# A two-layer block, attention and routed experts in float32: the last three weight passes walked once per 128-token tile

## The reference

```python
def mixer_sublayer(h, w_in, ...):
    proj = h @ w_in                    # 2048 x 7176
    sb_q, sb_k, sb_v, fq, fk, fv, fgate, flogit = jnp.split(proj, ...)
    sb = stick_breaking_attention(...)      # 8 heads of 128, causal
    fox = forgetting_attention(rms_norm(fq), rms_norm(fk), fv, log_f)  # 8 heads, causal
    merged = jnp.concatenate([rms_norm(sb, sb_out_gain),
                              rms_norm(fox, fox_out_gain) * jax.nn.sigmoid(fgate)], axis=-1)
    return merged @ w_out              # 2048 x 2048
...
def peer_sublayer(h, w_query, sub_keys, u, v):
    def block(hb):                     # 128 tokens
        q = (hb @ w_query).reshape(PEER_BLOCK, PEER_HEADS, 2, D_KEY // 2)   # 2048 x 2048
        s = jnp.einsum('thpc,hpnc->thpn', q, sub_keys)
        top_s, top_i = lax.top_k(s, PEER_TOPK)
        ...                            # 16 experts of 16384 for each token and head
        u_sel = jnp.take(u, idx, axis=0)
        a = jax.nn.gelu(jnp.einsum('thkd,td->thk', u_sel, hb), approximate=False)
        v_sel = jnp.take(v, idx, axis=0)
        return jnp.einsum('thk,thkd->td', g * a, v_sel)
    return lax.map(block, blocks)
```

## Time and profile before

| | before |
|---|---|
| time, median of 3 runs | 3122.51 us (3119.54, 3122.51, 3128.95) |
| span of the profiled execution | 3121.8 us |
| busy: TensorE, VectorE, ScalarE, GpSimd | 2089.0, 1836.5, 853.8, 800.9 us |
| second w_in (p4), loads issued | from 1141.1 us, for 508 us |
| query pass (p6), loads issued | from 1739.3 us, for 122 us |
| first gather of experts | 1797.4 us |
| last expert product on TensorE | starts at 3110.9 us |

### The profile page before, as it was taken

How to read it: one execution, slowest core, us unless ns; L and a number is a source line. 1 busy time by engine, 2 the same in 40 slices (tenths; PEclk the granted TensorE clock), 3 DMA queues, 4 the chain that set the end, 5 groups by cost and what they waited for, 6 DMA issues and landing times.

```text
span 3121.8 us, 29077 instructions
## 1 busy us (share of the span) xinstructions
PE 2089.0 (67%) x11378; PEld 1478.6 (47%) x11378; DVE 1836.5 (59%) x2711; ACT 853.8 (27%) x1267; POOL 800.9 (26%) x680
## 2 busy tenths in 40 slices
PE   5888989989999999999999983223232322322235
PEld 2676777888787787666668871000000000000001
DVE  3679886566776664343336697766565555564430
ACT  1334544444454454544545420000000000000000
POOL 1111110000000000000000036665555555555552
PEclk8999999999999999999999996566656566666667
DMA  9887875557665545334226699999999999999998
GB/s 385 289 293 263 296 259 150 184 182 248 210 189 153 164 158 172 111 122 132 85 82 201 194 377 403 422 422 421 421 422 421 422 421 419 421 421 421 421 421 346
DMA packets 244741, 900.90 MB, mean 289 GB/s; under 512 B 20759, under 2 KB 45613, under 8 KB 178413
## 3 DMA queue, kind: packets, MB, share of 16 engines
q0 software_dynamic: 94208, 612.85, 48.9%
q1 hardware_dynamic: 149152, 284.53, 27.8%
q10 hardware_dynamic: 1244, 1.67, 0.2%
HBM read 894.78 MB, written 2.10 MB: 287 GB/s over the span
## 4 chain that ended last, share of the span: by engine, by line
PE 45%; DMA 29%; DVE 10%; ACT 3%; issue 3%; POOL 2%; ACTq 0%; POOLq 0%; DVEq 0%
PE pp L1818 38%; DMA late<-in_peer_v,MI 9%; DMA P<-in_peer_v,MI 5%; PE tp L1818 5%; DMA x<-in_peer_v,MI 5%; DMA ring<-in_peer_v,MI 4%; DVE wL L1130 3%; DMA SY<-in_peer_v,MI 2%; PE tp L1821 2%; ACT wH L626 1%; DMA ring<-in_peer_w_query 1%; DVE UHM L1286 1%; DMA ring<-in_w_in 1%; POOL late L2361 1%; DVE P L1777 0%
## 5 line engine op out<-in xcount | busy, mean ns | idle before, releaser
L1130 DVE TENSOR_TENSOR wL<-ring,wH 128x1024 fp32r<-128x1024 f32 (+3 forms) x504 | 583.2, 1161 | 573.7 <-ACT wH L626 572.4
L1818 PE MATMUL pp<-wH,hH 128*128 128x512 f32 (+3 forms) x1888 | 745.7, 395 | 35.5 <-DVE wL L1130 19.4
L1818 PE MATMUL pp<-wL,hH 128*128 128x512 f32 (+3 forms) x1888 | 721.4, 382 | 0.0
L1818 PE MATMUL pp<-wH,hL 128*128 128x512 f32 (+3 forms) x1888 | 720.5, 382 | 0.0
L626 ACT ACTIVATE wH<-ring 128x1024 fp32r<-128x1024 f32 (+3 forms) x504 | 508.3, 1011 | 729.7 <-PE pp L1818 548.0
L1818 PE MATMUL pp<-late,S 128*32 128x512 f32 x768 | 232.6, 879 | 335.7 <-DMA x<-in_peer_v,MI 156.3
L1818 PEld LDWEIGHTS pp<-wH,hH 128*128 128x128 f32 x1888 | 362.3, 192 | 141.2 <-issue 46.3
L1818 PEld LDWEIGHTS pp<-wH,hL 128*128 128x128 f32 x1888 | 361.6, 192 | 64.1
L1818 PEld LDWEIGHTS pp<-wL,hH 128*128 128x128 f32 x1888 | 362.8, 192 | 57.3 <-issue 1.0
L1777 DVE CUSTOM_DVE_ANT_0 late<-late,P 128x2048 f32<-128x2048 f32 x84 | 191.2, 2288 | 155.2 <-DMA late<-in_peer_u,MI 155.2
L1818 PE MATMUL pp<-P,S 128*32 128x512 f32 x360 | 162.7, 898 | 166.9 <-DMA late<-in_peer_v,MI 93.2
(11 more groups left out here) (305 smaller groups left out, 2985.2 us busy)
## 6 DMA issues: line engine op xcount, KB each, us to landing
ring<-in_w_in SPq DMA_DIRECT2D x288, 512.0 KB, 4.4
ring<-in_w_out SPq DMA_DIRECT2D x96, 512.0 KB, 4.2
P<-in_w_mod POOLq DMA_DIRECT2D x85, 512.0 KB, 5.1
late<-in_w_mod SPq DMA_DIRECT2D x64, 512.0 KB, 9.4
SY<-in_w_mod POOLq DMA_DIRECT2D x43, 512.0 KB, 5.5
ring<-in_w_in SPq DMA_DIRECT2D x48, 368.0 KB, 4.8
ring<-in_peer_w_query SPq DMA_DIRECT2D x32, 512.0 KB, 7.9
ring<-in_w_in SPq DMA_DIRECT2D x24, 344.0 KB, 3.2
```

What stands on the lines that cost most here:

```text
L1130: tt(lo, raw, hi.bitcast(F32), ALU.subtract).then_inc(*tick("dve_lo", *names))
L1818: return e.matmul(o, l, r, start=start, stop=stop, skip_group_check=skip)
```

## The change

The first block stays. In the second block, tile 0 and tile 1 part:

- **Pass 1** (p4 to p6) computes only tile 0 (and the meta tokens). Pieces are now 128 rows of up to 1024 columns: still 512 KB, in rows of 4 KB. Of every four pieces of 128 rows one (`pc % 4 == 2`) is plain: TensorE reads it as float32 from the ring, against unsplit activations `hP` in `P`. The other three are split as before. A plain piece's ring buffer is free only when TensorE has used it.
- **Pass 2** (p7 to p9) loads w_in, w_out and the query matrix again, for tile 1, and every piece is plain. The tile's keys, values and activations are computed here; ScalarE and VectorE split no weights.
- **Beside pass 2** stand the 128 gathers and dots of tile 0's u, in 6 slots: `dot(SHARE)` after each piece adds 0.68 of a gather. The choices of groups 0 to 3 are laid into pass 2's attention. The rest of the experts (128 gathers of u for tile 1, 256 of v) comes after pass 2, in 13 slots.
- The attention code works tile by tile, so tile 0's queries meet one tile of keys. The sub-key load (2 x 512 KB) is done twice.

The core of the diff:

```diff
-G_IN2 = cgroups((FG + 688, 1, 344), *[(c + 512 * h, 1, 512) for h in range(2) for c in (SQ, SK, SV, FQ, FK, FV)],
-                (FG, 2, 344))
-GROUPS = [G_IN, G_OUT, G_IN, G_OUT, G_IN2, G_OUT, G_OUT]
-PIECES = [[(n, c0, w, pc) for n, (c0, w) in enumerate(g) for pc in range(8)] for g in GROUPS]
-NB, NS, NG = 3, 4, 11
-FIRST_DOT = 12
+G_IN2 = [(FG + 688, 344), (FQ, 1024), (FK, 1024), (FV, 1024), (FG, 688), (SQ, 1024), (SK, 1024), (SV, 1024)]
+G_OUT2 = [(0, 1024), (1024, 1024)]
+GROUPS = [G_IN, G_OUT, G_IN, G_OUT, G_IN2, G_OUT2, G_OUT2, G_IN2, G_OUT2, G_OUT2]
+BOTH = 4
+NPC = [8] * BOTH + [16] * 6
+PIECES = [[(n, c0, w, pc) for n, (c0, w) in enumerate(g) for pc in range(NPC[p])] for p, g in enumerate(GROUPS)]
+NB, NS, NG = 3, 4, 13
+SHARE = 0.68
...
+def row_of(p, n, pc):
+
+    return (pc + 8) % 16 if (p in (4, 7) and n == 7) or (p in (5, 8) and n == 0) else pc
+
+
+def plain(p, q):
+
+    return p >= 7 or (p >= BOTH and PIECES[p][q][3] % 4 == 2)
...
+    dots, chosen = [0, 0.0], [0]
+
+    def dot(share):
+        dots[1] += share
+        while dots[1] >= 1:
+            dots[1] -= 1
+            if dots[0] < 32 * min(chosen[0], 4):
+                yield "dot", dots[0] // 32, dots[0] % 32
+                if dots[0] >= 32 and dots[0] % 32 == 3:
+                    yield "gelu", dots[0] // 32 - 1
+                dots[0] += 1
...
+    for p in (4, 7):
+        t, share = tile_of(p), 0 if p == 4 else SHARE
+        for q, (n, c0, w, pc) in enumerate(PIECES[p]):
+            yield from splits(p, q)
+            if p == 4:
+                if n == 0 and pc == 4:
+                    yield "norm", 4
+                if n and pc == 3:
+                    yield "drain", "M"
+                if meta_part(c0, w):
+                    yield "meta", p, q
+            elif n == 0 and pc in (1, 2, 4, 6):
+                yield ("turn_q", 6, 1) if pc == 1 else ("scores", pc // 2)
+            elif (n, pc) in ((1, 2), (1, 14), (2, 10)):
+                yield from choice({(1, 2): 2, (1, 14): 3, (2, 10): 4}[n, pc])
+            if p == 7 and (n, pc) == (0, 8):
+                yield from choice(1)
+            yield "piece", p, q
...
+            yield from pump(*((0.8, 0.8, 1) if p == 4 else (0.7, 0.7, 1)))
+            yield from dot(share)
...
+                for k in range(14 if t else 0):
+                    yield "step", "X"
+                    yield "step", "Y"
+                    yield from dot(1)
+                yield "drain", "X", "Y"
...
+    yield "rest",
+    yield "turn_q", 9, 1
+    yield "scores", 6
+    yield "scores", 7
+    yield "open", "X", "choose", 4
+    yield "blend", 0
+    for b in range(8):
+        yield "vmix", 0, b
+        yield from dot(4)
+        yield from pump(1.5, 0, 0)
+    while dots[0] < 128:
+        yield from dot(1)
+        yield from pump(1, 0, 0)
+    yield "gelu", 3
...
-            had, queue = {}, [0, 1, 2, 3, 4]
-            for n in range(512):
-                if n == 34 - FIRST_DOT:
-                    queue = list(range(5, NG)) + queue
-                i = queue.pop(0)
-                queue.append(i)
-                yield i, had.get(i)
-                had[i] = n
+            had, queue, n = {}, [0, 1, 2, 3, 4, 5], 0
+            for what, *a in order():
+                if what == "rest":
+                    queue = list(range(6, NG)) + queue
+                for _ in range({"dot": 1, "vmix": 4}.get(what, 0)):
+                    i = queue.pop(0)
+                    queue.append(i)
+                    yield i, had.get(i)
+                    had[i] = n
+                    n += 1
...
+                    if p < BOTH:
+                        load(W[p][pc * 256:(pc + 1) * 256, c0:c0 + wd].rearrange("(k p) n -> p k n", p=128), 2, wd)
+                    else:
+                        k = row_of(p, n, pc)
+                        load(W[p][k * 128:(k + 1) * 128, c0:c0 + wd].unsqueeze(1), 1, wd)
...
+            def piece_one(p, q):
+                n, c0, wd, pc = PIECES[p][q]
+                whole, r, kk = plain(p, q), raw_of[p, q], row_of(p, n, pc)
+                k = None if whole else next(cut)
+                w.wait_ge(*(at("raw", r) if whole else at("lo", k)))
+                w.wait_ge(*(at("plain", p, kk // 4) if whole and p < 7 else at("chunk", p, kk // 4)))
+                h = hP if p < 7 else hB
+                for j, (o, wj) in enumerate(sides(wd)):
+                    b = bank_of(p, n, j)
+                    if pc == 0 and b in had_bank:
+                        w.wait_ge(*at(*had_bank[b]))
+                    if not whole:
+                        m = three(pp[b][:, 0:wj], (hA[0][:, kk, :], hA[1][:, kk, :]),
+                                  (wH[k % NB][:, o:o + wj], wL[k % NB][:, o:o + wj]), pc == 0, pc == 15)
+                    else:
+                        m = mm(pp[b][:, 0:wj], h[:, kk, :], ring[:, r % NS, o:o + wj], pc == 0, pc == 15)
+                    names = []
+                    if o + wj == wd:
+                        if not whole:
+                            names.append(("cut used", k))
+                        elif not (p == 4 and meta_part(c0, wd)):
+                            names.append(("ring used", r))
+                    if pc == 15:
+                        names.append(("grouped", p, n, j))
+                        had_bank[b] = ("bank free", p, n, j)
+                    m.then_inc(*tick("pe_piece", *names))
...
                 if before is not None:
                     w.wait_ge(*at("expert used", before))
-                elif slot in (3, 4):
+                elif slot < 6:
+                    w.wait_ge(*at("grouped", 6, 1, 1))
+                elif slot in (7, 8):
+                    w.wait_ge(*at("fox out", 1, 0, 1))
+                    w.wait_ge(*at("fox out", 1, 1, 1))
+                elif slot in (9, 10):
                     w.wait_ge(*at("turned x"))
-                    w.wait_ge(*at("hidden", slot - 3))
-                elif slot == 5:
-                    w.wait_ge(*at("lo", LAST_CUT))
-                elif slot == 7:
-                    w.wait_ge(*at("grouped", 6, 3))
+                    w.wait_ge(*at("hidden", slot - 9))
+                else:
+                    w.wait_ge(*at("grouped", 9, 1, 1))
...
```

More of the change, by code:

```diff
@@ L620, in split @@
                 n, c0, wd, pc = PIECES[p][q]
-                r, k = next(loads), next(cut)
-                raw = heads(ring[:, r % NS, 0:2 * wd], 2)
+                r = next(loads)
+                if plain(p, q):
+                    return
+                k, size = next(cut), 2 * wd if p < BOTH else wd
                 w.wait_ge(*at("raw", r))
@@ L988, in forget @@
[L988 to L999 removed]
+                half = meta[1]
@@ new lines, in turn_four @@
+                u = next(turn)
+                w.wait_ge(*at("turned", u))
+                if t == 0:
+                    act(mkt[:, 0 if names == "stick" else 1, 4 * half:4 * half + 4, :], heads(tp[u % 2][:, 512:576], 4), ACT.Copy,
+                        scale=kk).then_inc(*tick(R.act))
+                act(R.H[:, 512:1024 + 512 * t], tp[u % 2][:, 0:512 + 512 * t], ACT.Copy, scale=kk).then_inc(
+                    *tick(R.act, ("pair free", u), (names + " keys", *meta)))
+                yield
@@ new lines, in stick_a, with stick_v @@
+                act(z, z, ACT.Exp).then_inc(*tick(R.act))
+                w.wait_ge(*at("stick log", t, half, g, 1))
+                act(zm, zm, ACT.Exp).then_inc(*tick(R.act, ("stick weights", t, half, g)))
+                yield
+            def stick_v(lane, half, t, g):
+                R, hg = ROOM[lane], 4 >> t
+                yield
+                u = next(turn)
+                w.wait_ge(*at("turned", u))
+                o = YS + (4 * half + hg * g) * 128
+                act(P[:, t, o:o + hg * 128], tp[u % 2][:, 0:hg * 128], ACT.Copy).then_inc(
+                    *tick(R.act, ("pair free", u), ("mixed heads", t, half, g)))
+                yield
@@ new lines, in stick_a, with stick_v @@
+                yield
+                yield
+                u = next(turn)
+                w.wait_ge(*at("turned", u))
+                w.wait_ge(*now(R.dve))
+                tt(z, z, tp[u % 2][:, 0:512], ALU.subtract).then_inc(*tick(R.dve, ("stick log", t, half, g, 0)))
+                tt(zm, zm, tp[u % 2][0:16, 512:512 + hg * 128], ALU.subtract).then_inc(
+                    *tick(R.dve, ("pair free", u), ("stick log", t, half, g, 1)))
+                yield
+                yield
+            def stick_v(lane, half, t, g):
+                yield
+                next(turn)
+                yield
@@ L2319, in tensor @@
                     w.wait_ge(*at("blended", i))
+                    if b == 0 and i == 0:
+                        for n in range(2):
+                            for j in range(2):
+                                w.wait_ge(*at("bank free", 9, n, j))
                     if i == 4:
```

1283 lines of the change are left out of this document (632 added, 651 removed).

## The result

The changed kernel took 3233.7 us (median of 4 runs, 3230.1 to 3243.7) against 3121.0 before (median of 4, 3112.3 to 3129.0): a ratio of 1.037 with a 95% interval from 1.034 to 1.040. It is slower by 113 us; 3105 was forecast. Two executions of one kernel further down, the one with early gathers and deep rings, fell into a slow state at 3974 and 4530 us; they are left out of its time, and since the 4530 is its profiled one, no stage is read from that kernel.

What follows compares the result with a forecast made beforehand. w_in was taken as bound by TensorE and the expert stage by DMA, barely overlapping. Start 1157.5 + pass 1 395 + pass 2 582 + tail 970 gave 3104.5, forecast as 3105 us, range 3035 to 3185.

Steps and rivals of the forecast that it cites:

- the tail: After pass 2: 384 remaining gathers at 2.49 us each, 956 us, plus start and end, 970 us.
- (4.3 + 2.3) / 4 = 1.65 us: Pass 1: median load landing plus landing-to-release time of a split piece, over four buffers, taken as time per full piece.
- The price of 0.227: TensorE: split products of 512 columns start 0.227 us apart in the mean, three per 128 rows and tile, 0.68 us.
- a rival on the clock: Pass 2: lower TensorE clock costs 5 us at 0.75, total 3212 at 0.5; chance 0.05 together with no overlap.
- bound by the ring: Pass 1: late or plain pieces hold buffers; at 2.0 us a piece pass 1 is 455, total 3165; chance 0.11.
- 4 KB rows ran at 408 GB/s: Pass 2: 92.3 MB of weights at this rate take 226 us; with 319 us of gathers, 545 if never idle.
- 37 of slack: Pass 2 over 545 us: 5% over saturation gives 572, plus 7 at the query pass's end and 3 at the start, 582.
- 4 KB rows move at 330: Pass 2, named sign of being wrong: weight rows at 330 and not 408 GB/s would add 54 us.
- The starving rival: Pass 2: VectorE's order and six slots starve the DMA queues, share below 0.9; at 650 us total 3172; chance 0.18.
- The rule of turns among queues: Pass 2: DMA engines take packets in turn from queues, so weights get half of 408 GB/s, a load every 2.6 us.
- The two slow rivals: Pass 2 starves the DMA queues (3172 us, chance 0.18); pass 1 is bound by its ring buffers (3165 us, chance 0.11).
- The last rival: Pass 2: gathers hardly run there, pass 2 about 390 and tail up to 1275, total 3232; chance 0.05 together with clock.

Runs made afterwards that it cites:

- the one with early gathers and deep rings: Changed kernel with eight ring buffers in pass 1, six in pass 2, sub-keys turned later, gathers of v before pass 2's end: 3121.8 us, ratio to before 0.9996.
- the kernel with gathers behind: Against the changed kernel, all 128 gathers of tile 0 follow pass 2 instead of running beside it: total 3349 us, pass 2 429 us.
- filling the hole at the end: Against the changed kernel, GpSimd goes on with gathers of v in eight slots before pass 2 ends: total 3232 us, pass 2 647 us.
- deeper rings: Against the changed kernel, eight ring buffers in pass 1, six in pass 2's w_in and w_out, sub-keys turned three pieces later: 3126.5 us, ratio to before 1.000.

## Why the prediction was wrong

**What bounds the kernel before, and the tail: right.** 2.49 us a gather held (974.5 us for a forecast of 970), and so did the start.

**Pass 1: the failed step is the period "(4.3 + 2.3) / 4 = 1.65 us", taken as a rate.** In w_in both terms were right: with all pieces split, a load landed after 4.4 to 4.5 us and its wL ended 2.35 us later, in the median (3.2 in the mean). But loads and TensorE's other work don't overlap further than four buffers reach. Six and eight buffers bring 470 down to 416 and 394 with the same instructions on every engine; that is shown. Behind w_in the period itself was too short. In the query pass of the changed kernel the loads took 2.1 us each and not 1.65,

```profile
1546.15 65.83 SPq L667 DMA_DIRECT2D ring<-in_peer_w_query  x32
```

and in the kernel with all pieces split, where they took as long, each was issued at once when its buffer came free: they landed after 5.1 us, and wL ended 3.1 us later in the median and 3.8 in the mean. By the times of SyncE's loads, w_in took 315 us for 275, w_out 92 for 63 and the query pass 68 for 58.

Of the 75 us, by the timeline, 25 were more idle time than the sum held (63 for 38), 36 split and plain products that stood further apart (268 us for 232), and 14 the rest of TensorE's work, chiefly the small products of w_out and the query pass, which the sum left out. Of the 36, some 13 stand in the 64 split products that ran while 1.2 GHz was granted, 0.43 us apart. Some 11 stand in the first product of a run of split ones, after a wait or a product of another kind:

```profile
1491.25 0.48 PE L1914 MATMUL pp<-wH,hH 128*128 128x512 f32 x1
1491.57 0.40 PE L1914 MATMUL pp<-wL,hH 128*128 128x512 f32 x1
1491.80 0.40 PE L1914 MATMUL pp<-wH,hL 128*128 128x512 f32 x1
```

The first costs 0.32 us here and 0.34 in the median, its followers 0.23. The price of 0.227 came from the kernel before, where the same passes have 24 products in a run in the mean; here they have 9. Even with eight buffers the 720 products took 184 us and not 163, so this part is a price that was too low and not the ring. I had a rival on the clock, but only for pass 2. The rival on pass 1, "bound by the ring", was right in its name and its sign (pass 1 ending after 1600 us), and of its reasons the late piece that holds the next loads; the hold of plain pieces alone is not shown. Its price of 455 doesn't come out of its own figures: 2.0 in place of 1.65 us for the 96 full pieces without meta products adds 34 us to 395, which gives 429.

**Pass 2: the failed step is "4 KB rows ran at 408 GB/s", in the sum of 545 us.** 630 us at 366 GB/s are 231 MB, 4 more than counted. The share of 0.94 leaves 592 us of full queues; the forecast had 545 and 37 of slack, and 38 of slack there were. In 1700 to 1993, at a share of 0.99, the queues (packets, MB, share; q0 the gathers, q1 the weights) read:

```profile
q0 software_dynamic: 9575, 69.66, 57.6%
q1 hardware_dynamic: 13512, 46.46, 41.7%
```

Over 293 us that is 413 GB/s for gathers and 380 for weights. At these rates the bytes of the sum take 568 us and not 545, and the 4 MB some 10 more; the remaining 14 us are not placed. The prediction named the case "4 KB rows move at 330": alone, in pass 1 (202 GB/s at 0.61) and in the kernel with gathers behind (225 at 0.68), it is 331. The 2 KB rows of the kernel before gave 330, too, so the length of the rows was not what set 408 apart. I had it from a stretch with more loads in flight than four buffers allow; in it 46 loads left in 60 us and landed after 9.3 us, so that about seven were under way:

```profile
late<-in_w_mod SPq DMA_DIRECT2D x46, 512.0 KB, 9.3
```

The starving rival (650 us) had its length nearly right and its share (below 0.9) wrong. One slot less cost 6 us, but its other half, attention steps that wait behind dots, is there in TensorE's wait of 25 us, and no run took it out alone. The rule of turns among queues (the Trainium skill, page DMA: Bandwidth & Descriptors, section Queues, rings and completion order) was read as half of 408 GB/s for the weights, a load per 2.6 us. 10.4 us for four buffers is the same, but the rate is not: 46.46 MB in 293 us are 159 GB/s, a load per 3.3 us, since SyncE can load a buffer again only after its use, and the use comes after the landing. I wrote that the sum stays as it is, since 436 us are below 572; 160 loads at 3.3 us are 528, and the gathers' pace hangs on the pieces'. The prediction's 3.2 us for a load rest on a figure that the Trainium skill (same page, section Anatomy of one DMA) gives for transfers issued by GpSimd; these are issued by SyncE.

What stays open is how pass 2's 629 us divide between full queues, the ring and the wait behind the dots. Fewer gathers, six buffers, or filling the hole at the end each moved it by 6 to 18 us, in both directions, and the rate per share rose with deeper rings (381 GB/s at 0.96, against 366 at 0.94). No run separates them. Nor was the kernel before run with a deeper ring, so what depth alone would give it is not known.

**The chances.** The two slow rivals were weighed as alternatives, 3165 and 3172. They have separate causes, so they can come together, and the range ended at 3185. Their sum, 60 + 68 us over the forecast, is 3233, what was measured, but that match is luck: the stages were 75 and 47 us over. The last rival's 3232 is luck, too. It had hardly any gather in pass 2, and all 128 were there.

**The rest of the sum** was sound: with deeper rings the passes take 394 + 605 = 999 us against 977, and the kernel stands where 3105 + 22 puts it, level with before. Level is also what the idea is worth there: in the changed kernel 470 + 629 = 1099 us stand where 640 + 319 = 959 stood, 140 more, and only some 30 of them come back at the start of the tail; with deeper rings it is 40 more, most of which comes back.

## What to carry to other kernels

A ring of buffers is priced by the longest time in which its consumer does something else, not only by landing time over buffers: lay the consumer's bursts beside the ring's depth. A price read from the middle of a long run of products is too low where the runs get short. A transfer put "under" a stage that itself lives on loads is hidden only in part, here 37% of its time; measure that share before moving hundreds of them. Rivals with separate causes add up, and the range must reach their sum.

## What the runs showed of the hardware

The same 512 KB loads with 4 KB rows moved 331 GB/s per full DMA share with four buffers and no other traffic, 380 beside gathers, and 396 (408 at a share of 1.03) where about seven were in flight. A busy share near 0.6 was thus no sign of 40% to spare at the full rate. TensorE's granted clock stayed at 1.00 over 70 us in which it was busy 56, with 13 waits of at most 2.7 us, and went to 0.73 and 0.66 in windows of 10 us at and behind a single wait of 5.4 us. Split products of 512 columns stood 0.23 us apart within a run at 2.4 GHz, 0.43 at 1.2, and the first of a run cost about 0.34 at 2.4 GHz.
